# Raw residual into three projections, with 1/rms applied where they leave PSUM

## The reference, cut to what matters

```python
n = rms_norm(h, attn_norm[1])                 # second attention
q, k, v = split(n @ w_qkv); q, k = rope(q), rope(k)
...
x = rms_norm(h, final_norm)                   # end of the first block
hn = rms_norm_2(x, norm1_g[l])                # each latent mixer
proj = hn @ w_in                              # c_q 256, c_kv 128, k_r 32, stick q/k/v 768, pool 256
q = rms_norm_2(c_q) @ w_uq; kv = rms_norm_2(c_kv) @ w_ukv; k_rope = rope(k_r)
x = x + mixed @ w_out
x = x + hier_moe(rms_norm_2(x, norm2_g[l]))
```

## Time and profile before

| | |
|---|---|
| median of 3 runs | 1396.44 us (1394.47 to 1398.13) |
| profiled execution, its own time | 1396.2 us |
| span of the profile | 1394.2 us |
| PE busy | 1286.8 us, 92% |
| DVE, ACT, POOL busy | 662.3, 548.2, 36.7 us |
| chain that ended last, by engine | PE 76%, DVE 7%, DMA 7%, ACT 5%, issue 2% |

### The profile page before, as it was taken

How to read it: one execution, slowest core, us unless ns; L and a number is a source line. 1 busy time by engine, 2 the same in 40 slices (tenths; PEclk the granted TensorE clock), 3 DMA queues, 4 the chain that set the end, 5 groups by cost and what they waited for, 6 DMA issues and landing times.

```text
span 1394.2 us, 19006 instructions
## 1 busy us (share of the span) xinstructions
PE 1286.8 (92%) x7252; PEld 932.3 (67%) x7252; DVE 662.3 (48%) x1321; ACT 548.2 (39%) x1072; POOL 36.7 (3%) x75
## 2 busy tenths in 40 slices
PE   7999899999996899999899789999879987999986
PEld 5878899997875799999777544344357874443432
DVE  6656666666757566666666621111056463110102
ACT  5455544445445554444656311111044641111101
POOL 0000000000003000000200000000000000000000
PEclk9999999999999999999999999999999898999999
DMA  9532455554550265555432969999974096999995
GB/s 344 182 121 91 139 190 184 181 181 151 181 181 1 92 210 182 186 187 185 139 122 105 378 256 423 420 420 421 422 264 153 23 387 228 416 422 421 421 421 232
DMA packets 68570, 336.80 MB, mean 242 GB/s; under 512 B 7888, under 2 KB 8016, under 8 KB 47376
## 3 DMA queue, kind: packets, MB, share of 16 engines
q1 hardware_dynamic: 68400, 335.50, 64.2%
q0 software_dynamic: 96, 0.30, 0.1%
HBM read 334.72 MB, written 1.05 MB: 241 GB/s over the span
## 4 chain that ended last, share of the span: by engine, by line
PE 76%; DVE 7%; DMA 7%; ACT 5%; issue 2%; POOL 1%; SPq 1%; DVEq 0%; ACTq 0%; POOLq 0%
PE bank L1358 15%; PE bank L1360 15%; PE bank L1359 15%; PE bank L1649 13%; DMA expert_part<-stream 7%; PE bank L1676 6%; PE bank L1606 2%; DVE w_low L815 2%; PE bank L1495 1%; ACT tok L497 1%; PE bank L1689 1%; ACT w_high L487 1%; ACT probs L533 1%; PE bank L1434 1%; PE bank L1410 1%
## 5 line engine op out<-in xcount | busy, mean ns | idle before, releaser
L815 DVE TENSOR_TENSOR w_low<-raw,w_high 128x1024 fp32r<-128x1024 f32 (+1 forms) x246 | 285.5, 1211 | 131.3 <-ACT w_high L487 131.0
L487 ACT ACTIVATE w_high<-raw 128x1024 fp32r<-128x1024 f32 (+1 forms) x246 | 241.6, 1042 | 43.6 <-PE bank L1360 43.2
L1649 PE MATMUL bank<-expert_part,slots_x 128*64 128x512 f32 x1024 | 233.0, 593 | 9.3 <-DMA expert_part<-stream 8.1
L1358 PE MATMUL bank<-x_high,w_high 128*128 128x256 f32 (+1 forms) x712 | 203.2, 285 | 3.8 <-DVE x_low L834 3.5
L1359 PE MATMUL bank<-x_low,w_high 128*128 128x256 f32 (+1 forms) x712 | 202.7, 285 | 0.0
L1360 PE MATMUL bank<-x_high,w_low 128*128 128x256 f32 (+1 forms) x712 | 202.7, 285 | 0.0
L1649 PEld LDWEIGHTS bank<-expert_part,slots_x 128*64 128x64 f32 x1024 | 76.8, 137 | 159.0 <-issue 138.2
L1358 PE MATMUL bank<-w_high,x_high 128*128 128x512 f32 (+1 forms) x416 | 163.3, 393 | 5.1 <-DVE x_low L834 3.2
L1359 PE MATMUL bank<-w_low,x_high 128*128 128x512 f32 (+1 forms) x416 | 161.2, 387 | 0.0
L1360 PE MATMUL bank<-w_high,x_low 128*128 128x512 f32 (+1 forms) x416 | 160.9, 387 | 0.0
L1125 DVE SCALAR_TENSOR_TENSOR expert_hid<-expert_gate,combine,bank 128x256 f32<-128x256 f32 x32 | 15.4, 481 | 304.8 <-ACT expert_gate L640 304.8
(11 more groups left out here) (249 smaller groups left out, 1572.2 us busy)
## 6 DMA issues: line engine op xcount, KB each, us to landing
expert_part<-stream SPq DMA_DIRECT2D x164, 1024.0 KB, 17.9
raw<-stream SPq DMA_DIRECT2D x244, 512.0 KB, 5.2
expert_part<-stream SPq DMA_DIRECT2D x56, 512.0 KB, 17.8
const_sb<-const SPq DMA_DIRECT2D x1, 2070.0 KB, 13.4
residual<-x SPq DMA_DIRECT2D x2, 512.0 KB, 4.1
final_gain<-fgain SPq DMA_DIRECT2D x2, 512.0 KB, 8.8
out<-residual SPq DMA_DIRECT2D x2, 512.0 KB, 2.9
small_sb<-small SPq DMA_DIRECT2D x1, 765.0 KB, 5.9
```

The source lines that it names most:

```text
L487: nc.scalar.activation(wh[:, u, cols], raw[:, u, cols], ACT.Copy).then_inc(w_high, 1)
L815: tt(wl[:, u, cols], raw[:, u, cols], wh[:, u, cols].bitcast(F32), ALU.subtract).then_inc(w_low, 1)
L1358: mm(o, ah, bh, start=start, stop=False, **kw)
L1649: ins = mm(B[0][half * CAP:(half + 1) * CAP, :], xg[p // 4 % 2][:, k, x_of], w[k % 4 // 2][:, k % 2 * 512:(k % 2 + 1) * 512], start=k == 0 ...
```

## The change

1. Seam 1: PE transposes the residual itself, each half as soon as it is added. The squares of token tile 1 come after `high` on ACT. 1/rms is applied in `rope` (three products of each tile become scalar_tensor_tensor) and in `copy_v` (the scale of the activation).
2. Seam 2: likewise. The first mixer's gain is the product of the final gain of the first block and `norm1_g`, made once by DVE from a small transposed load of the final gain. DVE multiplies the residual by the final gain after its split of chunk c0+2, and by its 1/rms before the latent attention. The squares of the gained residual (`rms(5)`) stand on ACT between the splits of chunks c0+2 and c0+3.
3. Seam 3: likewise, with no gain in between. The first chunk of the second mixer is split beside the last expert pair.
4. In both FFNs DVE no longer splits the chunk two ahead before it adds the banks; that split comes after `low`.

```diff
             # SP, loads
                     load(c)
+                    if c == C_FFN[0]:
+                        columns = fgain[0][0:1, :].rearrange("o (k p) -> p (o k)", p=P)
+                        sync.dma_start(fg_col[:, :], columns, allow_slow_non_contiguous=True).then_inc(fg_col_in, 16)
             # POOL
+            def mixer_rms(l):
+                norm[0] += 1
+                for t in range(NT):
+                    pool.wait_ge(ssq_ready, 4 * norm[0] - 2 + 2 * t)
+                    eps = EPS if l else eps_ms[:, t:t + 1]
+                    link(nc.gpsimd.tensor_scalar(msq[:, t:t + 1], ssq[:, t, 0:1], ssq[:, t, 1:2], eps, ALU.add, ALU.add))
+                    nc.gpsimd.tensor_tensor(srs[:, t:t + 1], msq[:, t:t + 1], cs("minus_half", 0, 1), ALU.pow)\
+                        .then_inc(rstd_ready, 1)
+                    for j in range(2):
+                        ins = nc.gpsimd.tensor_scalar(eps_ms[:, 4 + 2 * t + j:5 + 2 * t + j], msq[:, t:t + 1], EPS, 0.0,
+                                                      ALU.mult, ALU.add)
+                link(ins)
             # ACT, last expert pair
+                    if p == NPAIR - 1 and l + 1 < LAYERS:
+                        split(S_LAYER[l + 1])
...
-                    split(S_LAYER[l + 1])
                     split(S_LAYER[l + 1] + 1)
             # ACT, seam 1
-            rms(2)
+            rms(2, False, range(2))
             high(T_L1, xh, lambda k: ps("attn_g", KT + k, KT + k + 1), C_DIFF)
+            rms(2, False, range(2, 4))
             # ACT, seams 2 and 3
-            rms(4)
...
-                rms(5 + 2 * l)
-                high(t_layer(l, 0), xh, lambda k: ps("norm1_g", l * KT + k, l * KT + k + 1), c0)
-                plain(c0, 2)
+                if l == 0:
+                    rms(4, False, range(2))
+                    high(t_layer(0, 0), xh, lambda k: first_gain[:, k:k + 1], c0)
+                    rms(4, False, range(2, 4))
+                    plain(c0, 1)
+                    act.wait_ge(rstd_ready, 10)
+                    rms(5)
+                    plain(c0 + 1, 1)
+                else:
+                    high(t_layer(l, 0), xh, lambda k: ps("norm1_g", l * KT + k, l * KT + k + 1), c0)
+                    rms(7)
+                    plain(c0, 2)
             # DVE, rope (scaled and the key part of the latent mixer likewise)
-                    tt(a, src, co, ALU.mult)
-                    tt(b[:, :, 0:32], src[:, :, 32:64], si[:, :, 0:32], ALU.mult)
-                    link(tt(b[:, :, 32:64], src[:, :, 0:32], si[:, :, 32:64], ALU.mult))
+                    by = None if scales is None else scales[:, t:t + 1]
+                    scaled_by(a, src, by, co)
+                    scaled_by(b[:, :, 0:32], src[:, :, 32:64], by, si[:, :, 0:32])
+                    link(scaled_by(b[:, :, 32:64], src[:, :, 0:32], by, si[:, :, 32:64]))
             # DVE, end of an FFN
-                plain(c0 + 3 * NFB - 1, 1)
                 c = c0 + 3 * NFB - 1
             # DVE, seam 1
-            normed(2)
             low(T_L1, xl, xh, lambda k: ps("attn_g", KT + k, KT + k + 1))
+            split(C_DIFF + 1)
+            dve.wait_ge(fg_col_in, 16)
+            tt(first_gain[:, :], fg_col[:, :], ps("norm1_g", 0, KT), ALU.mult).then_inc(gain_ready, 1)
             # DVE, last expert pair
+                    if p == NPAIR - 1 and l + 1 < LAYERS:
+                        split(S_LAYER[l + 1], 0, (0,))
...
+                        if p == NPAIR - 1 and half == 0 and l + 1 < LAYERS:
+                            split(S_LAYER[l + 1], 0, (1,))
             # DVE, seams 2 and 3
-            gained(4, 1)
...
                 if l:
-                    split(c0)
-                normed(5 + 2 * l)
-                if l:
+                    low(t_layer(l, 0), xl, xh, lambda k: ps("norm1_g", l * KT + k, l * KT + k + 1))
                     split(c0 + 1)
-                low(t_layer(l, 0), xl, xh, lambda k: ps("norm1_g", l * KT + k, l * KT + k + 1))
-                plain(c0, 4)
+                    plain(c0, 4)
+                else:
+                    dve.wait_ge(gain_ready, 1)
+                    low(t_layer(0, 0), xl, xh, lambda k: first_gain[:, k:k + 1])
+                    split(c0 + 1)
+                    plain(c0, 1)
+                    dve.wait_ge(fg_in, 16)
+                    dve.wait_ge(ssq_ready, 20)
+                    for t in range(NT):
+                        tt(h[:, t, :], h[:, t, :], fg[:, :], ALU.mult).then_inc(h_ready, 2)
+                    plain(c0 + 1, 3)
+                dve.wait_ge(rstd_ready, 2 * (5 + 2 * l) + 2)
                 dve.wait_ge(c_rstd_ready, l + 1)
...
                 stick_minus(2)
+                if l == 0:
+                    dve.wait_ge(ssq_ready, 24)
+                    for t in range(NT):
+                        ts(h[:, t, :], h[:, t, :], rstd[:, t:t + 1], None, ALU.mult)
             # PE
-            normed_transposes(T_L1)
+            normed_transposes(T_L1, 2)
...
-                normed_transposes(t_layer(l, 0))
+                normed_transposes(t_layer(l, 0), 7 if l else 4)
```

More of the change, by code:

```diff
@@ L257, in build @@
                 for i in range(SLOTS)]
-        over_chunk = [over(f"overflow_chunk{j}", [P, CH], F32, half_at[RING + j][0]) for j in range(3)]
+        over_chunk = [over(f"overflow_chunk{j}", [P, CH], F32, half_at[3 * RING + j][0]) for j in range(3)]
         tok_high = over("tok_high", [P, NT, D], F32R, v_at)
@@ L445, in _ @@
             rms()
+            link(nc.gpsimd.tensor_scalar(eps_ms[:, 0:NT], msq[:, 0:NT], EPS, 0.0, ALU.mult, ALU.add))
             for l in range(LAYERS):
@@ L487, in split, with rms @@
                     nc.scalar.activation(wh[:, u, cols], raw[:, u, cols], ACT.Copy).then_inc(w_high, 1)
-            def rms(additions, by_half=False):
+            def rms(additions, by_half=False, pieces=range(4)):
                 for i, (t, half) in enumerate(HALVES[by_half]):
+                    if i not in pieces:
+                        continue
                     if additions:
@@ L519, in qkT_copy, with copy_v @@
                         .then_inc(qkT_ready, 1)
-            def copy_v(c, banks, at, src=None):
+            def copy_v(c, banks, at, scale=None, norm=0):
                 act.wait_ge(chunk_used, c + 1)
+                if scale is not None:
+                    act.wait_ge(rstd_ready, 2 * norm + 2)
                 for t in range(NT):
-                    nc.scalar.activation(v[:, t, at:at + 512], B[banks + t][:, :], ACT.Copy).then_inc(v_ready, 1)
+                    nc.scalar.activation(v[:, t, at:at + 512], B[banks + t][:, :], ACT.Copy,
+                                         scale=1.0 if scale is None else scale[:, t:t + 1]).then_inc(v_ready, 1)
             def softmaxes(first, heads, between=None):
@@ L549, in head_squares, with projections @@
                     ins.then_inc(hss_ready, 1)
-            def projections(c0, qk_first, first):
+            def projections(c0, qk_first, first, scale=None, norm=0):
                 for g in range(6):
@@ L562, in projections @@
                     if g >= 4:
-                        copy_v(c + 1, 2 * (g % 2), 512 * (g - 4))
+                        copy_v(c + 1, 2 * (g % 2), 512 * (g - 4), scale, norm)
             def plain(c0, n):
@@ L732, in _ @@
                 plain(c0 + 4, 2)
-                copy_v(c0 + 5, 0, 512)
+                copy_v(c0 + 5, 0, 512, srs, 5 + 2 * l)
                 def stick(function, first, n, ready, done, x, **kw):
@@ L804, in link, with split @@
                 dve.wait_ge(dve_step, step[0])
-            def split(c, off=0):
+            def split(c, off=0, halves=range(2)):
                 u = c % RING
@@ L811, in split @@
                 n = WIDTH.get(c, CH) // 2
-                for half in range(2):
+                for half in halves:
                     cols = slice(half * n, half * n + n)
@@ L838, in one, with scaled_by, rope @@
                 return cs("ones", 0, 1)
-            def rope(n, c, banks, cos, sin):
+            def scaled_by(o, src, scale, table):
+                if scale is None:
+                    return tt(o, src, table, ALU.mult)
+                return stt(o, src, scale, table, ALU.mult, ALU.mult)
+            def rope(n, c, banks, cos, sin, scales=None, norm=0):
                 dve.wait_ge(chunk_used, c + 1)
+                if scales is not None:
+                    dve.wait_ge(rstd_ready, 2 * norm + 2)
                 for t in range(NT):
```

46 lines of the change are left out of this document (31 added, 15 removed).

## The result

The changed kernel took 1381.17 us (median of 5 runs, 1378.05 to 1384.74) against 1396.44: a ratio of 0.9892, interval 0.9875 to 0.9908, 15.3 us. The profiled execution took 1379.51 (span 1377.7), 16.5 less than the span of before.

What follows compares the result with a forecast made beforehand. PE, busy 92% of the span, was taken as the bound, so only its idle places at three seams could give time. Gains 2.2 + 3.5 + 5.4 = 11.1 us gave a median of 1385.3 us, range 1381.5 to 1390.5.

Steps and rivals of the forecast that it cites:

- Seam 1: After the first FFN: only the turn stays between PE's products, gain 2.4 us; rope hidden, copy_v costs 0.2, net 2.2.
- The split behind `low`: All seams: DVE's later split of the second chunk just meets PE's need; cost 0, up to 0.3 per latent seam.
- Seam 2, start: Into the first latent mixer: PE's first product comes 7.5 us sooner, with norms and DVE passes off the path.
- Seam 2, the new wait: First latent mixer: ACT's late squares delay DVE's splits and c_tok; PE resumes at X + 23.6, leaving 4.9 of 7.5 us.
- X: Time of PE's first product at seam 2 after the change, forecast at 675.7 us.
- the sum: Whole kernel: seam nets 2.2 + 3.5 + 5.4 = 11.1 us, taken from the profiled 1396.2 us.
- POOL's scale: First latent mixer: POOL's new operations end near X + 17, before DVE needs them at 20.9.
- Scaling: Before the first latent attention: DVE's two operations multiplying the residual by 1/rms cost 1.4 us, between 0 and 1.5.
- Seam 3: Into the second latent mixer: PE's first product 5.7 us sooner, additions about 0.15 later, `kr_tok` costs 0.3; net 5.4.
- The small load: SP's queue before the first FFN: 1024 four-byte pieces, taken as 0 cost; as the slower rival, near 1990 us, chance 0.03.
- The clock stays low: Rival at the seams: PE's clock still falls, costing 3.2 to 4.8 us in all, 1388.5 to 1390; chance 0.15.

Runs made afterwards that it cites:

- delayed_start: Changed kernel with SP loading the final gain first and awaiting it, so all work starts later (3.8 us): 1388.15 us, ratio 0.9935 to the kernel before.
- filler: Changed kernel plus five unread identity transposes before PE's wait for probabilities at every second head of the second attention: 1383.54 us, ratio 0.9911 to the kernel before.
- late scaling: Changed kernel with the residual's scaling by 1/rms moved from the first latent attention's start to behind head 5's scores: 1386.77 us, ratio 0.9960 to the kernel before.
- `c_tok` first: Changed kernel with DVE's split of the sixth chunk put behind c_tok and kr_tok in both latent mixers: 1386.88 us, ratio 0.9926 to the kernel before.
- before_again: The kernel before, run once more with no edit: 1396.68 us, ratio 1.0003.
- after_again: The changed kernel, run once more with no edit: 1380.08 us, ratio 0.9895 to the kernel before.

## Why the prediction was wrong

* **Seam 1**: right. 2.83 for 2.4, the copy of v 0.19 for 0.2; rope hidden.
* **The split behind `low`**: right, free at all seams.
* **Seam 2, start**: right, 7.90 for 7.5, at clock 1.00.
* **Seam 2, the new wait**: right in place, PE resumes at X + 23.0 for X + 23.6, so the wait cost 2.0 for 2.6. That the clock falls behind a wait of 2.73 was not in the sum and costs 1.6 more. Its cause was right: DVE's splits ahead of `c_tok`, late by ACT's order. `c_tok` ahead of the last split gave 2.3 us; moving ACT's squares brought the splits forward by 1.8, but POOL's scale, which the forecast had ready at X + 17 and free, then came last.
* **Scaling**: 1.14 for 1.4. **Seam 3**: 5.04 and 0.40 for 5.7 and 0.3; the gap from the first scatter shrank by 5.80, and the scatters came 0.76 later (forecast 0.15), 0.46 of it by the split beside the last pair, whose chunk landed late.
* **The small load**: it landed in 4.9 us and the first FFN ended at 338.22 for 338.14. Free.
* **The step that failed** is the sum itself: "2.2 + 3.5 + 5.4 = 11.1", taken from the profiled span with all other stretches as they were. They held 6.05 us of the profiled difference and, by the medians, 15.3 - 10.45 = 4.9. The clock stood in the text as a rival that could only cost ("The clock stays low", 1388.5 to 1390), and only at the seams. That it was already low in the kernel before at 485 and at 1105 us could be read in windows along the whole span; that this could go was not priced. A low end that gave back the falls of before would have held the result.

What the 4.9 us is owed to. Shown: it is clock, not another mechanism (same instructions, other granted clock, spans on one line against the clock; kernels with the same seams differ by it; a pure delay brings it back in delayed_start). Counted over the profiles: with the old seam 1 (five profiles) FFN 1 took 190.0 each time, with the new one 188.5 in seven of thirteen; with the old seam 3 (five) the heads of the second mixer took 27.27 to 29.55, with the new one 23.2 in six of thirteen. So the lower times came only with the new seams, and whether one gets them depends on small shifts of time. That seam 1 brings one and seam 3 the other is not shown, with five profiles on one side. What exactly decides a fall inside the heads stays open; the filler tried one cause and settled nothing, and fillers in the mixers' waits weren't tried.

## What to carry to other kernels

Split the time between milestones of the bottleneck engine before and after: stretches that an edit touches give its worth to some tenths, and stretches that it doesn't touch show what the clock did. Where the page shows the clock under full speed anywhere, a forecast needs a term for it in both directions, here some 6 us each way, as large as seam 3. An edit worth 1 to 4 us can't be judged by the median alone, as the late scaling and `c_tok` first show (5.6 and 5.7 us slower by the median, 1.1 and 3.9 faster in place). It can't be judged in place alone either: where the fall comes back in every profile, as with the late scaling, it is part of the edit's price. When a norm is taken off the path, look at which small result its consumers wait for next.

## What the runs showed of the hardware

* The falls repeat: before and before_again, after and after_again fall in the same places (442, 449, 695, 753, 790, 1138 us for the latter). The same work 3.8 us later has the falls from 442 to 801 us again, 4 us later, and a new one from 1095 to 1108 us.
* The long falls inside a mixer's heads, 17 in the 36 stretches of the profiles, all begin 12.7 to 14.7 us after the third turn. Their place in the work hardly moves; whether they come does.
* A wait of PE of 2.7 to 3.0 us before chunk c0+4 had a fall behind it in all ten profiles with such a wait; the waits of 0.4 to 1.7 us there had none in the eight others.
* A POOL operation on 128 x 1 took 0.37 us while DVE was idle and 2.03 and 2.47 while DVE ran its splits, subtractions of 128 x 1024 in SBUF. The Trainium skill (GPSIMD Engine Reference, Specifications) says that POOL's SBUF interfaces are shared with VectorE and contend with its operations that read two SBUF inputs; the trace agrees.
* Sixteen transposes of 128 x 128 behind a busy PE ran in 1.91 us at clock 1.00, at both seams.
* 1024 pieces of four bytes landed in 4.9 us, as soon as a half chunk of 512 KB in the same kernel (5.3).
